# Router by token in a hybrid encoder trunk: the RMS factor as a column, logits and turned tokens between the blocks of the output projection

## What is computed

```python
        h = h + hyena_mixer(...)                     # ends with  y @ w_out + b_out
        h = h + moe_swiglu(rmsnorm(h, norm_ffn_odd), moe_router, moe_w_gate, moe_w_up, moe_w_down)
    return rmsnorm(h, final_norm)[:, N_META:]

def rmsnorm(x, w):
    y = xf * lax.rsqrt(jnp.mean(xf * xf, axis=-1, keepdims=True) + EPS)
    return y.astype(x.dtype) * w.astype(x.dtype)

def moe_swiglu(x, router, wg, wu, wd):
    logits = (xt @ router).astype(F32)               # 256 tokens x 8 experts
    top_v, top_i = lax.top_k(logits, TOP_K)          # two experts a token
    wts = jax.nn.softmax(top_v, axis=-1)
    gates = jnp.sum(one_hot(top_i) * wts[..., None], axis=1)
    for e in range(N_EXPERTS):
        out = out + swiglu(xt, wg[e], wu[e], wd[e]) * gates[:, e:e + 1]
```

## Time and profile before

| | us |
|---|---|
| median of 3 runs | 1771.41 |
| lowest, highest | 1768.81, 1774.82 |
| the profiled execution, time | 1769.82 |
| the profiled execution, span | 1768.0 |
| TensorE busy in it | 1689.7 (96%) |
| mean granted TensorE clock | 0.952 |

### The profile page before, as it was taken

How to read it: one execution, slowest core, us unless ns; L and a number is a source line. 1 busy time by engine, 2 the same in 40 slices (tenths; PEclk the granted TensorE clock), 3 DMA queues, 4 the chain that set the end, 5 groups by cost and what they waited for, 6 DMA issues and landing times.

```text
span 1768.0 us, 22150 instructions
## 1 busy us (share of the span) xinstructions
PE 1689.7 (96%) x8381; PEld 1374.8 (78%) x8381; DVE 1251.2 (71%) x1179; ACT 991.1 (56%) x912; POOL 59.9 (3%) x54
## 2 busy tenths in 40 slices
PE   7998698999989999799999999999999999999996
PEld 5775368999928937678888888888888888888885
DVE  4356745555344733588898898888888988988883
ACT  2354434443234610377677767777677776777672
POOL 0132000000010020100000000000000000000000
PEclk8997688999998999799999999999999999999997
DMA  7331023557402503099999999999999999999981
GB/s 247 101 95 48 1 72 120 179 185 215 159 0 95 167 24 143 0 350 367 346 353 371 341 354 372 330 364 348 356 369 343 357 366 346 355 372 340 355 331 72
DMA packets 221092, 429.19 MB, mean 243 GB/s; under 512 B 9490, under 2 KB 76440, under 8 KB 220720
## 3 DMA queue, kind: packets, MB, share of 16 engines
q1 hardware_dynamic: 217528, 423.77, 67.8%
q10 hardware_dynamic: 3512, 4.73, 0.8%
HBM read 427.43 MB, written 1.05 MB: 242 GB/s over the span
## 4 chain that ended last, share of the span: by engine, by line
PE 91%; DVE 5%; ACT 2%; DMA 1%; issue 1%; ACTq 0%; DVEq 0%; SPq 0%
PE ps L1428 89%; PE ps L1440 2%; DVE arena L1043 1%; DVE ring_lo L1097 1%; ACT arena L562 1%; DVE arena L936 0%; DVE arena L1168 0%; DMA arena<-in_meta_tokens_dram 0%; DMA raw<-in_moe_w_gate_dram 0%; DMA raw<-in_moe_w_down_dram 0%; DVE w_lo L1236 0%; ACT ring_hi L719 0%; DVE arena L1171 0%; DVE rstd L942 0%; ACT arena L646 0%
## 5 line engine op out<-in xcount | busy, mean ns | idle before, releaser
L1236 DVE TENSOR_TENSOR w_lo<-raw,w_hi 128x2048 fp32r<-128x2048 f32 x224 | 511.9, 2292 | 80.3 <-ACT w_hi L830 76.1
L830 ACT ACTIVATE w_hi<-raw 128x2048 fp32r<-128x2048 f32 x224 | 428.9, 1919 | 182.4 <-DMA raw<-in_moe_w_gate_dram 97.5
L1428 PE MATMUL ps<-w_hi,xg_hi 128*128 128x512 f32 x896 | 355.1, 396 | 2.8 <-DVE xg_lo L1336 1.4
L1428 PE MATMUL ps<-w_hi,xg_lo 128*128 128x512 f32 x896 | 349.5, 390 | 0.0
L1428 PE MATMUL ps<-w_lo,xg_hi 128*128 128x512 f32 x896 | 349.3, 390 | 0.0
L1240 DVE TENSOR_TENSOR w_lo<-raw,w_hi 128x2048 fp32r<-128x2048 f32 x112 | 256.2, 2288 | 53.5 <-ACT w_hi L834 53.4
L834 ACT ACTIVATE w_hi<-raw 128x2048 fp32r<-128x2048 f32 x112 | 214.9, 1919 | 89.1 <-DMA raw<-in_moe_w_down_dram 87.2
L1428 PEld LDWEIGHTS ps<-w_hi,xg_hi 128*128 128x128 f32 x896 | 168.3, 188 | 37.0 <-DVE w_lo L1236 2.1
L1428 PEld LDWEIGHTS ps<-w_hi,xg_lo 128*128 128x128 f32 x896 | 168.2, 188 | 36.4
L1428 PEld LDWEIGHTS ps<-w_lo,xg_hi 128*128 128x128 f32 x896 | 168.5, 188 | 33.1
L1428 PE MATMUL ps<-w_hi,eh_hi 128*128 128x512 f32 x448 | 177.2, 395 | 7.6 <-DVE eh_lo L1329 7.1
(11 more groups left out here) (250 smaller groups left out, 2062.6 us busy)
## 6 DMA issues: line engine op xcount, KB each, us to landing
raw<-in_moe_w_gate_dram SPq DMA_DIRECT2D x112, 1024.0 KB, 5.2
raw<-in_moe_w_up_dram SPq DMA_DIRECT2D x112, 1024.0 KB, 5.3
raw<-in_moe_w_down_dram SPq DMA_DIRECT2D x112, 1024.0 KB, 5.0
ring<-in_w_in_ab_dram SPq DMA_DIRECT2D x12, 1024.0 KB, 5.3
ring<-in_hy_w_in_dram SPq DMA_DIRECT2D x12, 1024.0 KB, 5.2
ring<-in_ffn_w_gate_dram SPq DMA_DIRECT2D x11, 1024.0 KB, 5.3
ring<-in_ffn_w_up_dram SPq DMA_DIRECT2D x11, 1024.0 KB, 5.3
ring<-in_ffn_w_down_dram SPq DMA_DIRECT2D x8, 1408.0 KB, 6.8
```

The lines of the kernel that those rows point to most:

```text
L830: nc.scalar.activation(w_hi[:, j, :], raw[:, j, :], ACT.Copy).then_inc(sem("gu_high"), 1)
L1236: V.tensor_tensor(w_lo[:, j, :], raw[:, j, :], w_hi[:, j, :].bitcast(F32), ALU.subtract).then_inc(sem("gu_split"), 1)
L1428: return nc.tensor.matmul(o, l, r, start=start, stop=stop)
```

## The change

Per projection tile VectorE now also writes `xw`, `hT` times the norm's weights without the RMS factor (into unused columns of the weight ring), and for tiles 2 to 5 splits one of the units 0 to 3. TensorE turns `xw` channel by channel (`turn_channel`), makes the logits from `xw` (`score_channel`) and sums the squares by token with `sq` as the stationary side and one column of `ones` moving (`sum_channel`): channels 0 and 1 are turned behind block 1; 2 and 3 turned and 0 to 3 scored and summed behind block 2; 4 and 5 behind block 3, then 6 and 7. The root and the reciprocal are of 128x2 (`rs`). `rs` scales the logits, and scales the turned rows where ScalarE copies them from PSUM (`scale=`); for the second half VectorE makes `xtk_lo` from PSUM. The ranking is made for both token tiles at once, the places lose two small instructions, the gates and the later table move behind `select(0)`, and the first gather uses `xtk_hi` and `xtk_lo` as the others do. `rt` shrinks from 1024 to 576 columns.

```diff
@@ tile_order
-    add("ho", 0, 8)
+    add("ho", 0, 6)
+    add("xk", 0, 2)
+    add("ho", 6, 2)
+    add("xm", 0, 2)
+    add("logit", 0)
     add("ss4", 0)
-    add("xk", 0, 2)
-    add("logit", 0)
-    add("xk", 2, 2)
     add("pos", 0)
@@ gpsimd
-            for k in range(4):
-                pool.wait_ge(used("xk"), k + 1)
-                at = (slice(None), k % 2, slice(512 * (k // 2), 512 * (k // 2) + 512))
+            for tt in range(2):
+                pool.wait_ge(used("xk"), tt + 1)
+                at = (slice(None), tt, slice(0, 512))
@@ scalar
                 squares("ho", "squares4", k, slice(META, T))
-                if k in (5, 6):
-                    high_gu(k - 5, 0)
+                if 2 <= k < 6:
+                    high_gu(k - 2, 0)
             t = ready(act, "ss4", 0)
-            a(nc.scalar.activation(rstd[:, 0:SEQ], t[:, 0:SEQ], ACT.Sqrt, bias=eps[:, 0:1], scale=1.0 / D), used("ss4"))
+            a(nc.scalar.activation(rs, t[:, 0:2], ACT.Sqrt, bias=eps[:, 0:1], scale=1.0 / D), sem("row_root"))
             a(nc.scalar.activation(crd[:, 10:11], eps[:, 0:1], ACT.Exp))
...
+            act.wait_ge(sem("row_rstd"), 1)
+            for tt in range(2):
+                at = (slice(None), tt, slice(0, 512))
+                t = ready(act, "xk", tt)
+                a(nc.scalar.activation(xtk_hi[at], t[:, :], ACT.Identity, scale=rs[:, tt:tt + 1]))
+                a(nc.scalar.activation(xtk[at], t[:, :], ACT.Identity, scale=rs[:, tt:tt + 1]), used("xk"))
+            for tt in range(2):
+                a(nc.scalar.activation(xtk_hi[:, tt, 512:1024], ready(act, "xm", tt)[:, :], ACT.Identity, scale=rs[:, tt:tt + 1]), sem("xm_high"))
+            act.wait_ge(sem("logit_shift"), 1)
+            a(nc.scalar.activation(rt[:, 32:48], rt[:, 16:32], ACT.Exp), sem("gate_exp"))
@@ vector
             for j in range(8):
                 t = ready(dve, "ho", j)
-                if j == 7:
-                    low_gu(0, 0)
                 mult_add(hT[:, j, META:T], t[:, 0:SEQ], par[:, C_BOUT + j:C_BOUT + j + 1], hT[:, j, META:T], used("ho"), ALU.add, ALU.add)
-            norm("ss4", C_NFO, slice(META, T), sem("xn4_ready"))
-            low_gu(1, 0)
+                v(V.tensor_scalar(xw[j], hT[:, j, META:T], par[:, C_NFO + j:C_NFO + j + 1], None, ALU.mult), sem("xw_ready"))
+                if 2 <= j < 6:
+                    low_gu(j - 2, 0)
...
+            dve.wait_ge(sem("row_root"), 1)
+            v(V.reciprocal(rs, rs), sem("row_rstd"))
             t = ready(dve, "logit", 0)
-            v(V.tensor_copy(lg, t[:, 0:16]), used("logit"))
+            v(V.tensor_tensor(by_tok(lg), by_tok(t[:, 0:16]), over_e(rs), ALU.mult), used("logit"))
...
+            v(V.tensor_tensor(gt_, l_f, l_e, ALU.is_gt))
+            v(V.tensor_tensor(eq_, l_f, l_e, ALU.is_equal))
+            v(V.tensor_tensor(eq_, eq_, tri2, ALU.mult))
+            v(V.tensor_tensor(gt_, gt_, eq_, ALU.add))
+            v(V.tensor_reduce(by_tok(rank), gt_, AX.X, ALU.add))
+            v(V.tensor_scalar(pick, rank, 1.5, None, ALU.is_lt), sem("pick_ready"))
+            v(V.tensor_reduce(m1[:, 0:2], by_tok(lg), AX.X, ALU.max))
+            v(V.tensor_tensor(by_tok(sh), by_tok(lg), over_e(m1[:, 0:2]), ALU.subtract), sem("logit_shift"))
             for tt in range(2):
...
+                dve.wait_ge(sem("xm_high"), tt + 1)
+                t = ready(dve, "xm", tt)
+                v(V.scalar_tensor_tensor(out=xtk_lo[:, tt, 512:1024], in0=t[:, :], scalar=rs[:, tt:tt + 1], in1=xtk_hi[:, tt, 512:1024].bitcast(F32),
+                                         op0=ALU.mult, op1=ALU.subtract), used("xm"))
...
             select(0)
...
+            v(V.tensor_scalar(flag, t[:, 16:24], float(CAP) + 0.5, None, ALU.is_gt), used("pos"))
+            dve.wait_ge(sem("gate_exp"), 1)
+            v(V.tensor_tensor(ex, ex, pick, ALU.mult))
...
+            select_gates(0)
...
                 gathered_low(i)
-                low_gu(2, S)
-                low_gu(3, S)
+                if first:
+                    later_table()
+                else:
+                    low_gu(2, S)
+                    low_gu(3, S)
@@ tensor
+            def turn_channel(k):
+                pe.wait_ge(sem("xw_ready"), k + 1)
+                for tt in range(2):
+                    group = "xk" if k < 4 else "xm"
+                    o = open_tile(group, tt) if k % 4 == 0 else ps[NUMBER[(group, tt)] % 8]
+                    last = turn(o[:, P * (k % 4):P * (k % 4) + P], xw[k][:, P * tt:P * tt + P])
...
+            def score_channel(k):
+                o = open_tile("logit", 0) if k == 0 else ps[NUMBER[("logit", 0)] % 8]
+                for tt in range(2):
+                    last = mm(o[:, NE * tt:NE * tt + NE], xw[k][:, P * tt:P * tt + P], router[:, k, :], k + tt == 0, k + tt == KT)
...
+            def sum_channel(k):
+                o = open_tile("ss4", 0) if k == 0 else ps[NUMBER[("ss4", 0)] % 8]
+                pe.wait_ge(sem("squares4"), k + 1)
+                for tt in range(2):
+                    last = mm(o[:, tt:tt + 1], sq[:, k, META + P * tt:META + P * tt + P], ones[:, 0:1], k + tt == 0, k + tt == KT)
...
             for b in range(4):
                 linear("ho", 2 * b, B_HO + b, xn, SEQ, coming=sem("yh_ready") if b == 0 else None)
-                if b:
-                    add_squares("ss4", "squares4", 2 * b - 2, 2, slice(META, T))
-            add_squares("ss4", "squares4", 6, 2, slice(META, T))
+                if b >= 1:
+                    for k in (2 * b - 2, 2 * b - 1):
+                        turn_channel(k)
+                if b >= 2:
+                    for k in ((0, 1, 2, 3) if b == 2 else (4, 5)):
+                        score_channel(k)
+                        sum_channel(k)
+            for k in (6, 7):
+                turn_channel(k)
+                score_channel(k)
+                sum_channel(k)
...
+            mm(o[:, 0:NE], US[:, 0, 0:P], pick[:, 0:NE])
+            for st in range(2):
+                mm(o[:, NE:2 * NE], US[:, st, P:2 * P], pick[:, NE * st:NE * st + NE], st == 0, st == 1)
...
@@ gather
-                        if isinstance(i, int):
-                            last = mm(o, xtk[:, tt, P * d:P * d + P], SEL[:, tt, :].bitcast(F32), tt == 0, tt == 1)
-                            continue
                         mm(o, xtk_hi[:, tt, P * d:P * d + P], SEL[:, tt, :], tt == 0, False)
                         last = mm(o, xtk_lo[:, tt, P * d:P * d + P], SEL[:, tt, :], False, tt == 1)
```

More of the change, by code:

```diff
@@ L296, in trunk @@
         gslot = sb("gslot", [P, 1])
-        rt = sb("rt", [P, 1024])
+        rt = sb("rt", [P, 576])
         xtk = sq[:].rearrange("p k t -> p (k t)")[:, 0:2 * D].rearrange("p (t d) -> p t d", t=2)
+        xw = [ring[:, k // 3, KT * 256 + SEQ * (k % 3):KT * 256 + SEQ * (k % 3) + SEQ] for k in range(KT)]
+        rs = rt[:, 528:530]
         osb2 = raw[:, 0, :].rearrange("p (t d) -> p t d", t=2)
@@ L884, in item @@
                 gathered_high(i)
-                high_gu(2, S)
-                high_gu(3, S)
+                if not first:
+                    high_gu(2, S)
+                    high_gu(3, S)
                 for s in range(STAGES):
@@ L1274, in _ @@
[L1274 to L1281, removed]
+            gt_, eq_ = (rt[:, a:a + 128].rearrange("p (t e f) -> p t e f", t=2, e=NE) for a in (128, 256))
@@ L1283, in _ @@
             t = ready(dve, "pos", 0)
[L1284 to L1287, removed]
+            mult_add(place3[:, :, 0:NE], by_tok(t[:, 0:16]), 1.0, by_tok(pick), None, ALU.add, ALU.mult)
             def column(table, tt, i):
@@ L1303, in over_k @@
                 return a.rearrange("p (k e) -> p k e", k=1).to_broadcast([P, LATER, NE])
[L1305 to L1320, removed]
             def hidden(S):
@@ L1732, in _ @@
                 close(last)
+            def turn_channel(k):
[4 more added lines that the diff above has]
+                    last = turn(o[:, P * (k % 4):P * (k % 4) + P], xw[k][:, P * tt:P * tt + P])
+                    if k % 4 == 3:
+                        close(last)
+            def score_channel(k):
+                o = open_tile("logit", 0) if k == 0 else ps[NUMBER[("logit", 0)] % 8]
+                for tt in range(2):
+                    last = mm(o[:, NE * tt:NE * tt + NE], xw[k][:, P * tt:P * tt + P], router[:, k, :], k + tt == 0, k + tt == KT)
+                if k == KT - 1:
+                    close(last)
@@ L1733, in _ @@
+            def sum_channel(k):
+                o = open_tile("ss4", 0) if k == 0 else ps[NUMBER[("ss4", 0)] % 8]
+                pe.wait_ge(sem("squares4"), k + 1)
+                for tt in range(2):
+                    last = mm(o[:, tt:tt + 1], sq[:, k, META + P * tt:META + P * tt + P], ones[:, 0:1], k + tt == 0, k + tt == KT)
+                if k == KT - 1:
+                    close(last)
+            pe.wait_ge(sem("router_in"), 16)
             for b in range(4):
```

(28 more changed lines are left out.)

62 lines of the change are left out of this document (36 added, 26 removed).

## The result

The changed kernel takes 1776.11 us (median of 16 runs, 1774.09 to 1782.59) against 1770.86 for the kernel before in as many runs (1766.12 to 1776.06): 1.0035 of it, with a 95% interval of 1.0025 to 1.0045 (the quotient of the two medians is 1.0030). By the medians it is slower by 5.2 us, right at the bound of 0.3% that the prediction had drawn. The forecast was +4.4 us. The profiled execution of the changed kernel has a span of 1773.2 us, that of the kernel before 1768.0.

A forecast was written before the change was run, and what follows sets the result against it. TensorE bounds the experts; around the router a serial chain does. Projection +12.8 us, behind it -10.5, first stage +2.1: +4.4 on 1769.82, rounded to 1774 us; own range 1770 to 1778, for 8 in 10 1764 to 1782.

The forecast's parts named there:

- VectorE's rounds: Projection tiles 2 to 5: VectorE and ScalarE no longer overlap, 5.17 us a round against TensorE's 3.44 us a tile.
- TensorE's gap: Behind block 2: TensorE waits at `sum_channel(0)` for VectorE to evict tile 5, standing 4.8 us.
- The 28 small instructions at half clock: Left behind block 2 after TensorE's wait: 28 x 0.217 = 6.1 us, with 3.8 us as the lower bound.
- Block 3: Last projection block: 6.88 us at full clock, plus 2.3 for 4.6 us begun at half clock, ending at 727.6.
- The 40 small instructions: Between block 3 and the root: 3.3 us at full clock, the rest at half, 6.2 us.
- Root to first unit: Router chain through ScalarE's copies, VectorE's last subtraction, the gather (6.95 us) and splitting: 16.3 us.
- First unit: First split unit behind the router: at 750.2, 2.3 us later than before the change.
- First stage: First products of the experts, if the clock is still low: about 2.1 us lost, 0 at the other end.
- The likeliest class: Whole kernel: same time, a difference under 0.3% or 5.3 us; chance 0.52.
- rival C: Block 3: the clock isn't back within it, +11.5 us in all, 1781.3; chance 0.25, the full case less than half.
- B: Projection to router: the clock stays high or comes straight back, -6.7 us, 1763.1; chance 0.15.
- D: Projection: ScalarE's roundings run ahead of evictions, so TensorE doesn't stand; near -12 us, 1758; chance 0.03.

The follow-up runs named there:

- e8: Kernel before the change with nine, four and three unused matmuls in the router's waits for the norm, `pick` and `SEL`; 1766.62 us, 0.9982 of the kernel before.
- e1: Changed kernel with the splitting of units 0 to 3 put back where it was before the change; 1768.84 us, 0.9991 of the kernel before.
- e4: Changed kernel with ten unused matmuls of 256 columns ahead of `sum_channel(0)`, where TensorE stands; 1772.74 us, 1.0010 of the kernel before.
- e2: Changed kernel with VectorE's four subtractions one projection tile later, ScalarE unchanged; 1766.28 us, 0.9970 of the kernel before.
- e7: Changed kernel with only `sum_channel` of channels 0 to 5 moved behind block 3, splits still serial; 1764.32 us, 0.9974 of the kernel before.
- e5: e2 with six unused matmuls in TensorE's wait for `pick` and three in that for `SEL`; 1759.16 us, 0.9941 of the kernel before.
- e6: e2 with the Exp table load behind ScalarE's six scaled copies instead of ahead of them; 1765.05 us, 0.9972 of the kernel before.
- e10: e6 with GpSimd's two subtractions made by VectorE from PSUM, without ScalarE's two copies that fed them; 1766.70 us, 0.9970 of the kernel before.

## Why the prediction was right

Step by step, with the word of the prediction first:

- **VectorE's rounds.** 5.17 us from the earlier trace rows (the terms as written add up to 5.20); 5.25 and 5.18. TensorE's gap 4.8 (4.7 by its own times); 4.57.
- **The 28 small instructions at half clock.** 6.1 us; 6.0.
- **Block 3.** 9.2 us; 8.4 to the first turn. The clock was back 2.9 us into it (at 722.1), not 4.6; that is about the 2.8 that the earlier trace rows has as its shortest.
- **The 40 small instructions.** 6.2 us; 4.4. This term was mis-sized twice. The 0.135 us an instruction was the mean of a row of another stage, whose one-column instructions start unevenly, 0.11 to 0.18 us apart; here four take 0.445 us, 0.111 each. And the clock stayed at 1.00 over all forty, where the prediction counted on 3.3 us of that. The root came 1.8 us sooner behind block 3 than said.
- **Root to first unit.** 16.3 us; 16.5. It was ScalarE's copies and VectorE's last subtraction that stood in the chain, as the text had it, and the gather took 7.07 us at half clock throughout, 6.95 forecast. GpSimd's 1.28 us row was the right one to take: 1.28 and 1.26.
- **First unit.** +2.3 us was forecast; +0.68 was measured, and against the start of its projection -0.15.
- **First stage.** 2.1 us; G is 2.3 longer, and in the seven kernels whose first unit meets the low clock G is 111.3 to 112.3, in the four with the full clock 109.0 to 109.2, so about 2.7 on the average (e8, with its own stall, is left out). A second small wait of 0.36 us for unit 2 of the next stage belongs to it, which the text had not.

D and G give +2.2 us; the medians say +5.2, with 4.4 to 8.0 from the interval (0.25% to 0.45%). The forecast of +4.4 lies at its lower edge, and that was partly luck: block 3 and the 40 small instructions together were sized 2.6 us too high (0.8 and 1.8), and about as much came from elsewhere, 1.4 us of it from the stop in the last item, which the prediction hadn't and whose cause is open. The likeliest class was no change that can be told; the result stands on the edge of it, where the upper end of the forecast and rival C were given 0.30.

**The rivals.** B needed the clock to stay high or come back during small instructions. It did neither: in the changed kernel it was low over all 28 and came back only in block 3. Nor is the stall of 4.57 us needed for the fall: the clock fell during such instructions in e1 and e4, and 0.36 us behind them in e2, where no stall or only one of 0.35 us stood ahead. On the rule of the Trainium skill beside which B stood (TensorE: Matmul & The Clock Gate, What's actually happening), that the clock goes by how busy the engine has been: these rows don't bear it out if matmuls of one column, back to back, are read as a busy engine. C asked for block 3 wholly at half clock; it was low for 2.9 of 8.4 us. D, ScalarE running ahead, is what e2 built on purpose, by moving VectorE instead: it gives 7.4 us in D.

The prediction did not see that the same mechanism could be cured on either side (e2, e7), nor that the clock over the router was worth 6 us (e5); it had that only as the good end of a range.

## What to carry to other kernels

Before work is moved under a loop of tiles, write down for one tile what each engine's queue holds in order: if A's next item waits for B's last and B's next for A's, the two no longer overlap, and one tile of delay on one side (e2) restores it. Where PSUM tiles go round in numbered banks, a tile inserted ahead of others changes which eviction every later tile waits for; read the new n - 8. And where TensorE only waits or makes matmuls of a few columns, look at the granted clock of what comes next: a few large matmuls into a free bank, inside the wait and shorter than it, can be worth more than the order of the small ones.

## What the runs showed of the hardware

- Matmuls of 128 columns in fp32r, 32 in a row, did not bring the clock back in any of the seven kernels whose gather began low (in the changed one 0.50 over 6.9 us, 32 instructions at 0.217 us), while in the float32 ones of before it came back after 4.7 us (at 745.1). Where the added matmuls, 18 instructions of 256 columns in float32, stood in the two waits ahead of them (e5), it was at 1.00 throughout.
- In e1 and e2 the clock fell at the end of a run of 36 small instructions (4 turns, 32 of 1 and 8 columns, no gap of 0.3 us): in e1 0.45 us ahead of its end, in e2 0.36 us behind it (0.50 from 708.8 to 712.2 us). In the changed kernel it stayed at 1.00 over the 40 behind block 3 (4.4 us) and fell 0.3 us behind the last, in the wait that follows.
- A GpSimd subtraction of 128x512 from SBUF made VectorE's instructions on 16 elements last 1.06 and 1.22 us instead of 0.17, and without it they were short (e6, e10). The same shows in the kernel before: two `TENSOR_SCALAR` of line 1281 at 0.87 and 0.93 us beside GpSimd's second pair. The Trainium skill (SBUF — State Buffer, SBUF: two separate sides) says that GpSimd and VectorE take a shared pair of ports by an exclusive lock, for some kinds of VectorE instructions, and the other one waits for the whole instruction. The trace agrees: both end within 0.02 to 0.05 us of the subtraction's end.
